# Sliding-window attention: the two half-masked key blocks of a query row packed into one row of 128 columns

## The chip, the cores and the metric

The kernel runs on one core of a Trainium2 chip. The metric is the device time of one execution in microseconds (us), the median of three runs. TensorE is the matrix engine (PE in the rows; its weight loads are PEld), VectorE is DVE, ScalarE is ACT, GpSimd is POOL, and SP issues transfers.

## The reference, cut to what matters

The whole computation is two blocks of a network over 512 tokens of width 1024, in float32. The change touches one piece of it, the attention of the second layer (`swa_sink_mixer`), which has 16 query heads of width 64, 4 key heads, a window of 128 and one learned sink logit for each head:

```python
logits = jnp.einsum('bntgrd,bnsgd->bngrts', q, kk) * scale      # 128 queries x 256 keys
logits = logits + bias                                          # by distance, per head
logits = jnp.where(mask, logits, -jnp.inf)                      # 0 <= dist < 128
m = jnp.maximum(logits.max(-1), sink)
p = jnp.exp(logits - m[..., None])
denom = p.sum(-1) + jnp.exp(sink - m)
o = jnp.einsum('bngrts,bnsgd->bntgrd', p, vv) / denom
```

A block of 128 queries sees its own block of 128 keys (those at or before the query) and the block before it (those after the query's column). Of the 256 logits of a row exactly 128 are inside the window: column s of the own block where s <= t, and column s of the block before where s > t. The first block of queries has no block before it.

## The kernel before, in words

The engines run programs of their own, each strictly in the order written, and meet at semaphores. Most of the kernel is matrix products with weights that are streamed from memory in 118 chunks of 1 MB. Float32 operands are split into a high part (ACT, L1202) and a low part (POOL, L468 and L477, four pieces to a chunk), and each product is three matmuls (L503 to L505). Between these products stand two attentions.

The sliding-window attention works in 16 units. Unit i covers two heads (index x) and two query tiles of 128 (index t; tiles 0 and 1 in even units, 2 and 3 in odd ones), so a unit has four rows of logits, each of 256 keys, for every one of the 128 partitions. What each engine does for a unit:

- PE, `sw_score(i)`: logits into PSUM pair 0 (L917). There is one such pair, so the scores of a unit wait until the maximum of the unit before has been taken (`l_ready`).
- DVE, `sw_logits(i)`: scales and adds the bias, which holds the mask too (L2103, one instruction for each tile), after a memset of the block that tile 0 has not (L2099); then the maximum of each row (L2107).
- ACT, `sw_expo(i)`: four exponentials of 257 columns, the sink's column among them, with their sums (L1503). `sw_sink` puts the sink there (L1508).
- DVE, `sw_weights(i)`: reciprocal of the sums (L2112), four multiplications of 256 columns (L2115).
- PE, `sw_turn(i)`: eight transposes into PSUM pair 1 (L930).
- ACT: copies the transposed weights to `PT` (L1534).
- PE, `sw_weigh(i)`: weights times values (L944), 12 matmuls in even units and 16 in odd ones.
- DVE, `sw_finish(b)` after every second unit: two instructions that split the output (L2123, L2125).

PE's order is written out by hand. Round u has scores of unit u+2, then pieces of other matrix products (12 matmuls of 512 columns in rounds 1 to 9; six in rounds 11 to 14; 12 in round 15; here they are called the filling; in rounds 2 and 6 it stands behind the transposes), then the transposes of unit u, then the weighing of unit u-1. Round 10 has no filling. DVE's round i is `sw_logits(i+1)`, in odd rounds `sw_finish`, `sw_weights(i)`. ACT's round i is `sw_expo(i+1)`, in rounds 1, 5 and 9 the copy of new queries (L1514), the copy of `PT`, the sink of unit i+3, and in rounds 1, 5 and 9 the high part of a weight chunk (L1202).

The bias rows with the mask are made at the start of the kernel (L1697) and brought back as `BIAS` by a transfer from L1493.

Of the kernel before, what the change touches and what calls it, by code (L numbers as in the profile page):

```python
# [22 lines left out]
F32 = mybir.dt.float32  # L23
# [68 lines left out]
def build(nc, stream, x_t, mem_t, params, consts, masks, sinks, rel_in, w_pool, out):  # L92
    bias_rows = nc.dram_tensor("bias_rows", (P, SWH, 2 * P), F32).ap()
    forget_rows = nc.dram_tensor("forget_rows", (8, T), F32).ap()
    bias_toeplitz = bass.AP(bias_rows.tensor, 0, [[SWH * 2 * P - 1, P], [2 * P, SWH], [1, 2 * P]])
# [3 lines left out]
    with ExitStack() as ctx:  # L99
# [59 lines left out]
        with ExitStack() as s:  # L159
            REL = sb("REL", [BUCKETS, SWH + 2 * P], F32, s)  # L160
            ROWS = sb("ROWS", [SWH, 2 * P], F32, s)
            ROWM = sb("ROWM", [SWH, 2 * P], F32, s)
        with ExitStack() as s:
# [13 lines left out]
            with ExitStack() as s1:  # L177
                BIAS = sb("BIAS", [P, SWH, 2 * P], F32, s1)
# [3 lines left out]
                PL = sb("PL", [P, 3, 4, 2 * P + 8], F32, s1)  # L182
                PT = sb("PT", [P, 2, 8, P], F32, s1)
# [66 lines left out]
        def bk(i):  # L250
# [41 lines left out]
            sem(n) for n in ("s_mm", "l_ready", "p_exp", "p_ready", "p_turned", "pt_ready", "pv_mm"))  # L292

# [206 lines left out]
        def _(pe):  # L500
# [331 lines left out]
            pe.wait_ge(consts_in, 64)  # L832
# [101 lines left out]
            def sw_weigh(i):  # L934
# [4 lines left out]
                for t, n in enumerate(tiles):  # L939
                    nk = min(n + 1, 2)  # L940
                    for x in range(2):
                        for kb in range(nk):
# [3 lines left out]
                                           PT[:, i % 2, 4 * x + 2 * t + kb + 2 - nk], start=kb == 0, stop=kb == nk - 1)  # L946
# [248 lines left out]
        def _(act):  # L1195
# [27 lines left out]
            act.dma_start(ROWM[:, :], rel_in[BUCKETS:BUCKETS + SWH, SWH:]).then_inc(consts_in, 16)  # L1223
# [225 lines left out]
            def ffn(n_in, n_down, layer):  # L1449
# [14 lines left out]
                if layer == 1:  # L1464
# [3 lines left out]
                    act.dma_start(INV[:, :, :], consts[:, NCON:].rearrange("p (b t) -> p b t", b=2)).then_inc(inv_loaded, 16)  # L1468
# [22 lines left out]
            def load_bias():  # L1491
                act.wait_ge(rows_stored, 16)
                act.dma_start(BIAS[:, :, :], bias_toeplitz).then_inc(bias_loaded, 16)  # L1493

            layer_norm(1, par["ffn_g"][:, 0:8], par["ffn_b"][:, 0:8], load_bias)

            def sw_expo(i):
# [3 lines left out]
                for r in range(4):  # L1501
                    row = PL[:, s, r, 0:2 * P + 1]
# [3 lines left out]
            def sw_sink(i):  # L1506
                _, b, _ = SW_UNITS[i]
                act.activation(PL[:, i % 3, :, 2 * P].rearrange("p (x t) -> p x t", t=2),  # L1508
                               SINK3[:, b // 4, :, b % 4].unsqueeze(2).broadcast_to([P, 2, 2]), ACT.Copy).then_inc(sink_put, 1)

            def sw_query(c):
                pair = bank[1] if c == 0 else bank[3]
                act.wait_ge(w_used, SQ_CHUNK[c] + 1)
                act.activation(QB[:, 2 * c:2 * c + 2], pair[:, :, :], ACT.Copy).then_inc(qb_copied, 1)  # L1514
# [139 lines left out]
        def _(dve):  # L1654
# [40 lines left out]
            dve.wait_ge(consts_in, 64)  # L1695
            dve.wait_ge(rel_mm, 1)
            dve.tensor_tensor(ROWS[:, :], bk(7)[0:SWH, 0:2 * P], ROWM[:, :], ALU.add).then_inc(rows_made, 1)  # L1697
# [388 lines left out]

            BIAS5 = BIAS[:, :, :].rearrange("p (o x b) s -> p o x b s", o=2, x=2)

            def sw_logits(i):
# [37 lines left out]
            dve.wait_ge(bias_loaded, 16)  # L2127
# [307 lines left out]
```

## Time and profile before

| | |
|---|---|
| runs | 1485.28, 1484.1, 1484.4 us; median 1484.4 us |
| span of the profiled execution | 1483.1 us, first to last instruction |
| the profiled execution's own time | not shown apart from its span; the median of the runs is 1.3 us above that span |
| PE busy | 1452.5 us (98%) |
| DVE, ACT, POOL busy | 859.6, 615.7, 482.5 us |
| the 16 units on PE | from 695.84 us (first score) to 801.56 us (first matmul behind the last weighing) |

A row of the busy list gives a share of the whole span; a stage can have another limit than the whole. Matmuls are pipelined, so neighbouring ones overlap and the duration of one is more than its distance to the next.

### The profile page before, as it was taken

To read this page: it belongs to the slowest core of one execution; us is meant where nothing else is said; L and a number is where in the kernel's file an instruction comes from. 1 tells how busy PE (TensorE), PEld (TensorE's weight loads), DVE (VectorE), ACT (ScalarE), POOL (GpSimd) and SP (SyncE) were. 2 spreads that over 40 slices of the span, in tenths; PEclk is the share of its full clock that TensorE was granted. 3 is DMA by queue.
4 is the path that set the end of the run, shared out by engine and by line. 5 is a ranking of instruction groups with operands and counts; after the bars stand their busy time and mean duration, and the time that the engine had idled before them with its cause. 6 is when DMAs were issued, how large, how long until landed. Compare 5 with 4: busy or idle time off the path is not lost.

```text
span 1483.1 us, 23698 instructions
## 1 busy us (share of the span) xinstructions
PE 1452.5 (98%) x9390; PEld 1207.6 (81%) x9390; DVE 859.6 (58%) x1261; ACT 615.7 (42%) x780; POOL 482.5 (33%) x360
## 2 busy tenths in 40 slices
PE   8999999999999999999999999999999999999999
PEld 6787887898888888899777988888888897777677
DVE  7787686576665660165686666656630374565741
ACT  5565554353223221245574442232221355655541
POOL 0000000225544545432221145445454524422222
PEclk9999999999999999999999999999999999999999
DMA  7422122403222233323102122222323312322211
GB/s 222 136 74 87 58 86 102 156 29 114 85 92 106 87 112 113 112 87 106 66 30 86 57 86 85 95 103 88 110 85 112 129 58 86 130 74 71 72 56 59
DMA packets 23601, 137.25 MB, mean 93 GB/s; under 512 B 2600, under 2 KB 5208, under 8 KB 8672
## 3 DMA queue, kind: packets, MB, share of 16 engines
q1 hardware_dynamic: 18288, 124.79, 23.9%
q10 hardware_dynamic: 5232, 11.32, 2.8%
q8 instruction: 58, 0.95, 0.3%
q14 instruction: 23, 0.19, 0.0%
HBM read 131.89 MB, written 4.21 MB: 92 GB/s over the span
## 4 chain that ended last, share of the span: by engine, by line
issue 41%; PE 27%; POOL 24%; DVE 3%; DMA 2%; ACT 1%; DVEq 1%; POOLq 0%; ACTq 0%; SPq 0%
POOL WL L468 15%; POOL WL L477 9%; PE pair L503 7%; PE pair L505 6%; PE pair L504 6%; DMA RAW<-stream 1%; PE pair L1096 1%; PE pair L1083 1%; DVE WL L1672 1%; PE pair L688 1%; PE pair L1015 1%; PE pair L1073 1%; PE pair L717 1%; ACT WH L1202 1%; DMA PAR<-params 0%
## 5 line engine op out<-in xcount | busy, mean ns | idle before, releaser
L503 PE MATMUL pair<-AH,WH 128*128 128x512 f32 (+1 forms) x1240 | 473.4, 382 | 9.4 <-DVE AL L1661 6.6
L468 POOL TENSOR_TENSOR WL<-RAW,WH 128x512 fp32r<-128x512 f32 x228 | 310.5, 1394 | 475.6 <-ACT WH L1202 475.6
L505 PE MATMUL pair<-AH,WL 128*128 128x512 f32 (+1 forms) x1240 | 462.6, 373 | 0.0
L504 PE MATMUL pair<-AL,WH 128*128 128x512 f32 (+1 forms) x1240 | 462.4, 373 | 0.0
L1202 ACT ACTIVATE WH<-RAW 128x2048 fp32r<-128x2048 f32 x106 | 202.8, 1913 | 455.5 <-PE pair L505 446.4
L477 POOL TENSOR_TENSOR WL<-RAW,WH 128x512 fp32r<-128x512 f32 x128 | 171.8, 1374 | 506.8 <-ACT WH L1202 506.8
L503 PEld LDWEIGHTS pair<-AH,WH 128*128 128x128 f32 x1240 | 233.5, 188 | 58.5 <-issue 15.9
L505 PEld LDWEIGHTS pair<-AH,WL 128*128 128x128 f32 x1240 | 233.0, 188 | 41.8
L504 PEld LDWEIGHTS pair<-AL,WH 128*128 128x128 f32 x1240 | 233.5, 188 | 41.1 <-issue 1.9
L2042 DVE TENSOR_SCALAR CA<-pair,PAR 128x512 f32<-128x512 f32 x88 | 67.3, 806 | 147.4 <-PE pair L505 144.4
L503 PE MATMUL pair<-GH,WH 128*128 (+2 forms) x416 | 148.7, 357 | 0.1
L504 PE MATMUL pair<-GL,WH 128*128 (+2 forms) x416 | 147.7, 355 | 0.0
L505 PE MATMUL pair<-GH,WL 128*128 (+2 forms) x416 | 147.7, 355 | 0.0
L2047 DVE SCALAR_TENSOR_TENSOR CA<-pair,PAR,CA 128x510 f32<-128x510 f32 (+1 forms) x176 | 123.7, 744 | 14.0 <-issue 12.1
L503 PE MATMUL pair<-OH,WH 128*128 128x512 f32 (+1 forms) x256 | 89.4, 349 | 1.8 <-POOL WL L477 0.9
L503 PEld LDWEIGHTS pair<-GH,WH 128*128 128x128 f32 x416 | 78.1, 188 | 11.8 <-POOL WL L477 0.3
L505 PEld LDWEIGHTS pair<-GH,WL 128*128 128x128 f32 x416 | 78.4, 188 | 11.2
L504 PEld LDWEIGHTS pair<-GL,WH 128*128 128x128 f32 x416 | 78.1, 188 | 11.3
L504 PE MATMUL pair<-OL,WH 128*128 128x512 f32 (+1 forms) x256 | 86.1, 336 | 0.0
L505 PE MATMUL pair<-OH,WL 128*128 128x512 f32 (+1 forms) x256 | 86.0, 336 | 0.0
L1868 DVE TENSOR_TENSOR WL<-RAW,WH 128x1024 fp32r<-128x1024 f32 x16 | 22.4, 1444 | 99.5 <-ACT WH L1216 99.0
L503 PE MATMUL pair<-WH,AH 128*128 128x256 f32 (+1 forms) x192 | 59.7, 311 | 0.8 <-DVE AL L1952 0.6
(249 smaller groups left out, 1890.4 us busy)
## 6 DMA issues: line engine op xcount, KB each, us to landing
RAW<-stream SPq DMA_DIRECT2D x114, 1024.0 KB, 4.9
H<-x_t SPq DMA_DIRECT2D x5, 512.0 KB, 6.6
bias_rows<-ROWS ACTq DMA_DIRECT2D x1, 2048.0 KB, 24.5
BIAS<-bias_rows ACTq DMA_DIRECT2D x1, 2048.0 KB, 7.8
FBC<-forget_rows ACTq DMA_DIRECT2D x4, 512.0 KB, 4.0
out<-H ACTq DMA_DIRECT2D x8, 256.0 KB, 2.0
H<-x_t SPq DMA_DIRECT2D x1, 1024.0 KB, 10.4
RAW<-stream SPq DMA_DIRECT2D x3, 256.0 KB, 6.7
```

What stands on the lines that cost most here:

```text
L468: pool.tensor_tensor(WL[w][:, part], RAW[raw][:, part], WH[w][:, part].bitcast(F32), ALU.subtract).then_inc(w_lo, 1)
L477: pool.tensor_tensor(wl[:, :, part], raw[:, :, part], wh[:, :, part].bitcast(F32), ALU.subtract).then_inc(w_lo, 1)
L503: pe.matmul(out_, wh, xh, start=start, stop=False, skip_group_check=shared)
L504: pe.matmul(out_, wh, xl, start=False, stop=False, skip_group_check=shared)
L505: return pe.matmul(out_, wl, xh, start=False, stop=stop, skip_group_check=shared)
L688: mm = pe.matmul(out_[b:b + BLK, h, c * BLK:c * BLK + BLK], k_[:, b:b + BLK], q_[:, b:b + BLK], start=True, stop=True)
L717: mm = pe.matmul(pair_a[:, h, cs], vv[:, c, h * P:h * P + P], SS[:, h, c], start=c == 0, stop=True)
L1015: pe.matmul(bk(5), con["mean64"], SQH[:, :], start=True, stop=True).then_inc(n_summed, 1)
L1202: act.activation(WH[w][:, :], RAW[raw][:, :], ACT.Copy).then_inc(w_hi, 1)
L1868: dve.tensor_tensor(WL[w][:, part], RAW[w][:, part], WH[w][:, part].bitcast(F32), ALU.subtract).then_inc(e_lo, 1)
L2042: dve.tensor_scalar(out_[:, c], src[:, c], tap[2], CONVB[:, layer, ab, blk], ALU.mult, ALU.add)
L2047: ins = dve.scalar_tensor_tensor(out_[:, c, d:T], src[:, c, 0:T - d], CONVW[:, layer, 2 - d, ab, blk], out_[:, c, d:T], ALU.mult, ALU.add)
```

## The change

A query row keeps 128 columns from the start. ACT copies the own block's logits from PSUM to `PL` (`sw_own`), DVE overwrites the columns after the query with those of the block before (a predicated copy), and then the bias, the maximum, the exponential, the division and the transposes work on 128 columns. After the transpose the packed weights are spread again into two blocks, by a multiplication with two 0/1 masks (`sw_part`, on DVE, in place of ACT's copy). The transposes of neighbouring units go to two banks of pair 1 in turn. The scale moves to the copy of the queries. The bias loses its mask and half its columns; `PM`, the two masks, is a transfer more. Tile 0's missing block comes from the constant `causal`, whose masked columns hold -1e30.

```diff
             def sw_turn(i):
                 pe.wait_ge(p_ready, i + 1)
-                if i:
-                    pe.wait_ge(pt_ready, i)
-                for t in range(2):
-                    for x in range(2):
-                        for kb in range(2):
-                            at = 2 * t + kb
-                            mm = pe.transpose(bk(2 + x)[:, at * P:at * P + P],
-                                              PL[:, i % 3, 2 * x + t, kb * P:kb * P + P], con["ident"])
+                if i >= 2:
+                    pe.wait_ge(pt_ready, i - 1)
+                for r in range(4):
+                    mm = pe.transpose(bk(2 + i % 2)[:, r * P:r * P + P], PL[:, i % 3, r, 0:P], con["ident"])
                 mm.then_inc(p_turned, 1)
...
             def load_bias():
                 act.wait_ge(rows_stored, 16)
                 act.dma_start(BIAS[:, :, :], bias_toeplitz).then_inc(bias_loaded, 16)
+                act.dma_start(PM[:, :, :], consts[:, NCON + 2 * T:].rearrange("p (k t) -> p k t", k=2)).then_inc(bias_loaded, 16)
...
-                    row = PL[:, s, r, 0:2 * P + 1]
+                    row = PL[:, s, r, 0:P + 1]
...
-            def sw_sink(i):
+            def sw_own(i):
                 _, b, _ = SW_UNITS[i]
-                act.activation(PL[:, i % 3, :, 2 * P].rearrange("p (x t) -> p x t", t=2),
+                if i >= 3:
+                    act.wait_ge(p_turned, i - 2)
+                act.activation(PL[:, i % 3, :, P].rearrange("p (x t) -> p x t", t=2),
                                SINK3[:, b // 4, :, b % 4].unsqueeze(2).broadcast_to([P, 2, 2]), ACT.Copy).then_inc(sink_put, 1)
+                act.wait_ge(s_mm, i + 1)
+                own = bank[0][:, :, :].rearrange("p x (t k s) -> p (x t) k s", t=2, k=2)[:, :, 1]
+                act.activation(PL[:, i % 3, :, 0:P], own, ACT.Copy).then_inc(own_put, 1)
...
-            for i in range(3):
-                sw_sink(i)
+            sw_own(0)
             sw_expo(0)
+            sw_own(1)
...
             for i in range(16):
                 if i + 1 < 16:
                     sw_expo(i + 1)
+                if i + 2 < 16:
+                    sw_own(i + 2)
                 if i in (1, 5, 9):
                     sw_query((i + 3) // 4)
-                act.wait_ge(p_turned, i + 1)
-                if i >= 2:
-                    act.wait_ge(pv_mm, i - 1)
-                act.activation(PT[:, i % 2].rearrange("p (x k) c -> p x (k c)", x=2), bank[1][:, :, :], ACT.Copy).then_inc(pt_ready, 1)
-                if i + 3 < 16:
-                    sw_sink(i + 3)
-                if i in (1, 5, 9):
                     split_next(SQ_CHUNK[(i + 3) // 4])
...
             def sw_logits(i):
                 _, b, tiles = SW_UNITS[i]
-                s = i % 3
-                rows = PL[:, s].rearrange("p (x t) s -> p x t s", t=2)
-                nmax = NMAX[:, s].rearrange("p (x t) -> p x t", t=2)
-                bias = BIAS5[:, b // 4, :, b % 4]
+                rows = PL[:, i % 3, :, 0:P]
+                both = rows.rearrange("p (x t) s -> p x t s", t=2)
+                before = bank[0][:, :, :].rearrange("p x (t k s) -> p x t k s", t=2, k=2)[:, :, :, 0]
+                bias = BIAS5[:, b // 4, :, b % 4].unsqueeze(2).broadcast_to([P, 2, 2, P])
+                pair = LATER.unsqueeze(1).broadcast_to([P, 2, P])
                 dve.drain()
-                if i >= 3:
-                    dve.wait_ge(p_turned, i - 2)
+                dve.wait_ge(own_put, i + 1)
                 if tiles[0] == 0:
-                    dve.memset(rows[:, :, 0, 0:P], NEG)
-                dve.wait_ge(s_mm, i + 1)
-                for t in range(2):
-                    lo = P if tiles[t] == 0 else 0
-                    dve.scalar_tensor_tensor(rows[:, :, t, lo:2 * P], bank[0][:, :, 256 * t + lo:256 * t + 256], SCALE, bias[:, :, lo:],
-                                             ALU.mult, ALU.add)
+                    dve.copy_predicated(both[:, :, 0], pair, con["causal"].unsqueeze(1).broadcast_to([P, 2, P]))
+                    dve.copy_predicated(both[:, :, 1], pair, before[:, :, 1])
+                else:
+                    dve.copy_predicated(rows, LATER.unsqueeze(1).broadcast_to([P, 4, P]), before.rearrange("p x t s -> p (x t) s"))
+                dve.drain()
+                dve.tensor_tensor(both, both, bias, ALU.add)
                 dve.drain()
                 dve.wait_ge(sink_put, i + 1)
-                dve.tensor_reduce(nmax, rows[:, :, :, 0:2 * P + 1], AX_X, ALU.max, negate=True).then_inc(l_ready, 1)
+                dve.tensor_reduce(NMAX[:, i % 3], PL[:, i % 3, :, 0:P + 1], AX_X, ALU.max, negate=True).then_inc(l_ready, 1)
...
-                for r in range(4):
-                    ins = dve.tensor_scalar(PL[:, s, r, 0:2 * P], PL[:, s, r, 0:2 * P], RDEN[:, s, r:r + 1], None, ALU.mult)
-                ins.then_inc(p_ready, 1)
+                dve.tensor_tensor(PL[:, s, :, 0:P], PL[:, s, :, 0:P], RDEN[:, s].unsqueeze(2).broadcast_to([P, 4, P]),
+                                  ALU.mult).then_inc(p_ready, 1)
+
+            def sw_part(i):
+
+                dve.wait_ge(p_turned, i + 1)
+                if i >= 2:
+                    dve.wait_ge(pv_mm, i - 1)
+                turned = bk(2 + i % 2).rearrange("p (r t) -> p r t", r=4).unsqueeze(1).broadcast_to([P, 2, 4, P])
+                dve.tensor_tensor(PT[:, i % 2], turned, PM[:, :, :].unsqueeze(2).broadcast_to([P, 2, 4, P]),
+                                  ALU.mult).then_inc(pt_ready, 1)
...
             for i in range(16):
                 if i + 1 < 16:
                     sw_logits(i + 1)
+                if i:
+                    sw_part(i - 1)
                 if i >= 3 and i % 2:
                     sw_finish((i - 3) // 2)
                 sw_weights(i)
+            sw_part(15)
             sw_finish(7)
```

## Rows read from the trace of the kernel before

**Rows 1.** The page: the span, and busy time by engine.

```profile
span 1483.1 us, 23698 instructions
...
PE 1452.5 (98%) x9390; PEld 1207.6 (81%) x9390; DVE 859.6 (58%) x1261; ACT 615.7 (42%) x780; POOL 482.5 (33%) x360
```

**Rows 2.** Stretches: busy PE, PEld, DVE, ACT, POOL; then PE's granted clock, DMA.

```profile
775.00:785.00 10.00, 7.83 (x56) 5.80 (x56) 9.29 (x19) 6.71 (x22) 3.36 (x3) 1.00 0.30 107
785.00:795.00 10.00, 9.29 (x81) 6.87 (x80) 7.04 (x16) 6.98 (x20) 0.00 (x0) 1.00 0.21 65
```

**Rows 3.** Waits in 695 to 806 us: total us, times, longest.

```profile
DVE PL L2103 <- PE pair L917: 24.0, 6, 9.8
...
PE pair L930 <- DVE PL L2115: 2.7, 5, 1.4
```

**Rows 4.** Groups by line in 695 to 806 us: busy us, mean ns, idle before.

```profile
L1503 ACT ACTIVATE PL<-PL,SMALL 128x257 f32<-128x257 f32 x64 | 31.9, 500 | 5.2 <-DVE SMALL L2107 4.3
L2115 DVE TENSOR_SCALAR PL<-PL,SMALL 128x256 f32<-128x256 f32 x64 | 22.7, 418 | 1.2
...
L2107 DVE TENSOR_REDUCE SMALL<-PL 128x4 f32<-128x1028 f32 x16 | 19.6, 1224 | 1.5 <-issue 0.4
...
L2103 DVE SCALAR_TENSOR_TENSOR PL<-pair,BIAS 128x512 f32<-128x512 f32 (+1 forms) x32 | 18.3, 613 | 25.0 <-PE pair L917 24.0 <-issue 1.0
L930 PE MATMUL pair<-CON,PL 128*128 128x128 f32 x128 | 17.0, 276 | 2.7 <-DVE PL L2115 2.7
...
L1534 ACT ACTIVATE PT<-pair 128x1024 f32<-128x1024 f32 x16 | 16.3, 1021 | 22.1 <-PE pair L930 22.1
...
L1202 ACT ACTIVATE WH<-RAW 128x2048 fp32r<-128x2048 f32 x5 | 9.5, 1910 | 0.0
...
L2125 DVE TENSOR_TENSOR OL<-pair,OH 128x512 fp32r<-128x512 f32 x8 | 5.5, 692 | 0.6
```

**Rows 5.** Timeline, rounds 4 and 10 to 15: start us, length us, instruction, idle before.

```profile
736.51 0.50 PE L503 MATMUL pair<-AH,WH 128*128 128x512 f32 x1
...
739.37 1.04 PE L930 MATMUL pair<-CON,PL 128*128 128x128 f32 x8
...
771.06 0.93 PE L917 MATMUL pair<-KT,QB 64*128 64x128 f32 x8
771.07 1.14 DVE L2115 TENSOR_SCALAR PL<-PL,SMALL 128x256 f32<-128x256 f32 x4
...
772.39 0.27 DVE L2099 MEMSET PL<- 128x256 f32 x1 [0.18 <-issue]
...
774.98 1.13 PE L917 MATMUL pair<-KT,QB 64*128 64x256 f32 x8 [0.54 <-DVE SMALL L2107]
...
801.56 0.50 PE L503 MATMUL pair<-OH,WH 128*128 128x512 f32 x1
```

**Rows 6.** Timelines of POOL and of DVE around 726 us.

```profile
726.28 5.06 POOL L468 TENSOR_TENSOR WL<-RAW,WH 128x512 fp32r<-128x512 f32 x4 [11.48 <-ACT WH L1202]
...
729.00 3.02 DVE L2115 TENSOR_SCALAR PL<-PL,SMALL 128x256 f32<-128x256 f32 x4
```

**Rows 7.** Whole span, shapes apart: instructions of the kinds that the change adds.

```profile
L1894 DVE TENSOR_TENSOR SY<-SY,H 128x512 f32<-128x512 f32 x12 | 8.3, 692 | 1.0
...
L1780 DVE TENSOR_TENSOR E<-pair,E 128x1024 f32<-128x1024 f32 x4 | 4.9, 1224 | 9.8 <-ACT E L1245 9.8
...
L2234 DVE TENSOR_REDUCE SMALL<-PL 128x2 f32<-128x512 f32 x4 | 2.7, 686 | 0.3
...
L1755 DVE COPY_PREDICATED SB<-MASK,pair 128x256 f32<-128x256 uint32 x4 | 1.8, 450 | 0.1
...
L1554 ACT ACTIVATE PL<-PL,SMALL 128x128 f32<-128x128 f32 x8 | 3.1, 395 | 0.3
...
L1617 ACT ACTIVATE PT<-pair 128x512 f32<-128x512 f32 x4 | 2.4, 598 | 17.3 <-PE pair L1083 17.3
```

**Rows 8.** The page's transfers: KB of the bias transfer, us from issue to landing.

```profile
BIAS<-bias_rows ACTq DMA_DIRECT2D x1, 2048.0 KB, 7.8
```

More of the change, by code:

```diff
@@ L94, in build @@
     forget_rows = nc.dram_tensor("forget_rows", (8, T), F32).ap()
-    bias_toeplitz = bass.AP(bias_rows.tensor, 0, [[SWH * 2 * P - 1, P], [2 * P, SWH], [1, 2 * P]])
+    bias_toeplitz = bass.AP(bias_rows.tensor, P, [[SWH * 2 * P - 1, P], [2 * P, SWH], [1, P]])
     forget_bcast = [bass.AP(forget_rows.tensor, 2 * T * j, [[0, P], [T, 2], [1, T]]) for j in range(4)]
@@ L161, in build @@
             ROWS = sb("ROWS", [SWH, 2 * P], F32, s)
-            ROWM = sb("ROWM", [SWH, 2 * P], F32, s)
         with ExitStack() as s:
@@ L177, in build @@
             with ExitStack() as s1:
-                BIAS = sb("BIAS", [P, SWH, 2 * P], F32, s1)
+                BIAS = sb("BIAS", [P, SWH, P], F32, s1)
+                sb("BIAS_GAP", [P, SWH, P], F32, s1)
                 KT = sb("KT", [P, 2, T], F32, s1)
@@ L181, in build @@
                 QB = sb("QB", [P, 8, T], F32, s1)
-                PL = sb("PL", [P, 3, 4, 2 * P + 8], F32, s1)
-                PT = sb("PT", [P, 2, 8, P], F32, s1)
+                PL = sb("PL", [P, 3, 4, P + 8], F32, s1)
+                PM = sb("PM", [P, 2, P], F32, s1)
+                sb("PM_GAP", [P, 10 * P], F32, s1)
+                PT = sb("PT", [P, 2, 2, 4, P], F32, s1)
             with ExitStack() as s1:
@@ L292, in build @@
             sem(n) for n in ("s_mm", "l_ready", "p_exp", "p_ready", "p_turned", "pt_ready", "pv_mm"))
+        own_put = sem("own_put")
         n_squared, n_summed, n_rstd, n_made = (sem(n) for n in ("n_squared", "n_summed", "n_rstd", "n_made"))
@@ L831, in _ @@
             values(0, (0, 1, 2, 3))
-            pe.wait_ge(consts_in, 64)
+            pe.wait_ge(consts_in, 48)
             for it in range(4):
@@ L945, in sw_weigh @@
                                            VT[:, n + 1 - nk + kb, c0:c0 + 64],
-                                           PT[:, i % 2, 4 * x + 2 * t + kb + 2 - nk], start=kb == 0, stop=kb == nk - 1)
+                                           PT[:, i % 2, kb + 2 - nk, 2 * x + t], start=kb == 0, stop=kb == nk - 1)
                 mm.then_inc(pv_mm, 1)
@@ L1222, in _ @@
             act.preload_act_table_set("natural_log_exp_and_others")
-            act.dma_start(ROWM[:, :], rel_in[BUCKETS:BUCKETS + SWH, SWH:]).then_inc(consts_in, 16)
             act.dma_start(REL[:, 0:SWH], rel_in[0:BUCKETS, 0:SWH]).then_inc(rel_loaded, 16)
@@ L1467, in ffn @@
                         act.activation(MH[:, 4 * half:4 * half + 4], MT[:, 4 * half:4 * half + 4], ACT.Copy).then_inc(mh_ready, 1)
-                    act.dma_start(INV[:, :, :], consts[:, NCON:].rearrange("p (b t) -> p b t", b=2)).then_inc(inv_loaded, 16)
+                    act.dma_start(INV[:, :, :], consts[:, NCON:NCON + 2 * T].rearrange("p (b t) -> p b t", b=2)).then_inc(inv_loaded, 16)
                 split_next(n_down + 7)
@@ L1513, in sw_query @@
                 act.wait_ge(w_used, SQ_CHUNK[c] + 1)
-                act.activation(QB[:, 2 * c:2 * c + 2], pair[:, :, :], ACT.Copy).then_inc(qb_copied, 1)
+                act.activation(QB[:, 2 * c:2 * c + 2], pair[:, :, :], ACT.Copy, scale=SCALE).then_inc(qb_copied, 1)
             act.wait_ge(w_used, N_KV + 1)
@@ L1694, in _ @@
             dve.tensor_scalar(LB[:, 1], LB[:, 0], -1.0, 1.0, ALU.mult, ALU.add)
-            dve.wait_ge(consts_in, 64)
+            dve.wait_ge(consts_in, 48)
             dve.wait_ge(rel_mm, 1)
-            dve.tensor_tensor(ROWS[:, :], bk(7)[0:SWH, 0:2 * P], ROWM[:, :], ALU.add).then_inc(rows_made, 1)
+            dve.tensor_copy(ROWS[:, :], bk(7)[0:SWH, 0:2 * P]).then_inc(rows_made, 1)
             dve.drain()
@@ L2125, in sw_finish @@
                 dve.tensor_tensor(ol, o, oh.bitcast(F32), ALU.subtract).then_inc(o_ready, 1)
-            dve.wait_ge(bias_loaded, 16)
+            dve.wait_ge(bias_loaded, 32)
             sw_logits(0)
@@ L2320, in constants @@
 def constants():
-    c = np.zeros((P, NCON + 2 * T), np.float32)
+    c = np.zeros((P, NCON + 2 * T + 2 * P), np.float32)
     i = np.arange(P)
@@ L2336, in constants @@
     win = np.array(POOL_WINDOWS)[(i[:, None] // 64) + 2 * np.arange(2)[None]]
-    c[:, NCON:] = (1.0 / np.minimum(np.arange(T)[None, None] + 1, win[:, :, None])).reshape(P, -1)
+    c[:, NCON:NCON + 2 * T] = (1.0 / np.minimum(np.arange(T)[None, None] + 1, win[:, :, None])).reshape(P, -1)
+    c[:, NCON + 2 * T:] = np.concatenate([i[:, None] > i[None, :], i[:, None] <= i[None, :]], axis=1)
     masks = np.zeros((P, LEVELS - 1, P), np.float32)
@@ L2345, in constants @@
     j = np.arange(2 * P)
-    dist = P - j
-    ok = (dist >= 0) & (dist < P)
-    dc = np.clip(dist, 0, P - 1)
+    dc = (-j) % P
     d = np.maximum(dc, 1).astype(np.float32)
@@ L2351, in constants @@
     bucket = np.where(dc < 16, dc, np.minimum(log_b, BUCKETS - 1))
-    hot = ((bucket[None] == np.arange(BUCKETS)[:, None]) & ok[None]).astype(np.float32)
-    return c, masks, hot, np.where(ok, 0.0, NEG).astype(np.float32)
+    hot = (bucket[None] == np.arange(BUCKETS)[:, None]).astype(np.float32)
+    return c, masks, hot
 def kernel(**inputs):
@@ L2360 @@
     a = {k: np.asarray(v) for k, v in inputs.items()}
-    con, masks, hot, row_mask = constants()
+    con, masks, hot = constants()
     parts = []
@@ L2411 @@
     params = np.concatenate([vec[n] for n, _ in PARAMS], axis=1)
-    rel_in = np.zeros((BUCKETS + SWH, SWH + 2 * P), np.float32)
-    rel_in[0:BUCKETS, 0:SWH] = a["rel_bias"]
-    rel_in[0:BUCKETS, SWH:] = hot
-    rel_in[BUCKETS:, SWH:] = row_mask
+    rel_in = np.zeros((BUCKETS, SWH + 2 * P), np.float32)
+    rel_in[:, 0:SWH] = a["rel_bias"]
+    rel_in[:, SWH:] = hot
     w_pool = np.zeros((P, 2, P), np.float32)
```

1 line of the change is left out of this document (added).

## The prediction

> **What bounds the kernel.** I read the page first: PE is busy 98% of 1483.1 us, so as a whole the kernel is PE's [rows 1]. The change lies in one stage, so I then read stretches of that stage. There PE is not always full: 7.83 of 10 us from 775, while DVE has 9.29 [rows 2]; PE's granted clock is 1.00 in both, which is 2.4 GHz. The waits come next. For most of the stage DVE waits for scores (24.0 us [rows 3]) and ACT for transposes (22.1 us [rows 4]): PE sets the pace. But PE also waits for the weights that DVE makes, five times, 2.7 us in all [rows 3], and for the maximum, as in front of the scores of unit 13 [rows 5]. The reader is to see two parts. In rounds 0 to 9 PE has much filling and is the bound. From round 10 on the filling is thin and PE and DVE hold each other up. All idle time of PE in the stage is some 5.8 us, so that is the most that smoother waits could give; anything beyond must come out of PE's own work.
>
> **The terms on PE.** Eight transposes become four. The group L930 is busy 17.0 us for 16 units [rows 4], 1.06 us each; the last matmul lasts 0.28, so the distance from one to the next is (1.06 - 0.28) / 7 = 0.11 us. Four fewer save 0.44 us, 16 times: **-7.0 us**. Scores and weighing keep their number and size. That is what the change gives if nothing else becomes late.
>
> **The terms on ACT.** Exponentials: 257 columns take 0.50 us, 128 columns 0.395 [rows 4, 7]; four cost about 0.4 us less. The `PT` copy (1.02 us [rows 4]) leaves; a copy of 512 columns from PSUM (0.60 us [rows 7]) comes. ACT loses some 0.9 us a unit and is not the bound. But the new copy has a place in the chain: it stands behind `sw_expo(i+1)` (four pieces, 1.6 us), and in rounds 1, 5 and 9 the 1.9 us split of a chunk (L1202 [rows 4]) is also ahead of it.
>
> **The terms on DVE**, for a unit:
>
> - L2103 leaves, 18.3 / 16 = 1.14 us [rows 4], and the 0.18 us of the memset in even units [rows 5].
> - A predicated copy of 512 columns comes. The trace has it at 256 columns, 0.450 us [rows 7]. Other DVE kinds need 1.04 us for 1000 columns more: (1.224 - 0.692) / 512 [rows 7]. So 0.450 + 0.27 = **0.72 us**, and 0.81 in even units, where it is two of 256 (the second overlaps by 0.09). Bounds: not below 0.45, and 0.90 if it cost 256 twice in full.
> - The bias addition comes: 0.69 us, as L1894, and a drain of 0.07.
> - The maximum goes from 1.224 [rows 4] to 0.69 us (L2234 at 512 columns [rows 7]).
> - Four multiplications (1.14 us together [rows 5]) become one of 512 columns with two operands, 0.69 us.
> - `sw_part` comes: 1024 columns from PSUM with a second operand, as L1780, 1.224 us [rows 7]; it overlaps the instruction ahead by 0.09, so 1.13.
>
> Sum: out 1.14 + 0.09 + 1.22 + 1.14 = 3.59; in 0.76 + 0.76 + 0.69 + 0.69 + 1.13 = 4.03. DVE gets 0.44 us more in each unit, where PE gets 0.44 less. With reciprocal (0.17), drains and half of `sw_finish` (two of 0.69 us [rows 4]), DVE goes from 4.8 to 5.2 us a unit. PE's unit with full filling goes from 5.75 to 5.3 (scores 0.86 or 1.06, filling 2.84 (736.51 to 739.37 [rows 5]), transposes 0.97 to 0.53, weighing 0.86 or 1.07), and with six matmuls of filling from 4.4 to 3.9. So DVE comes level with PE in rounds 1 to 9, and is well above it from round 10.
>
> **Why the waits grow by more than the sums say.** The scores have one PSUM pair and wait for the maximum. Between one unit's scores and the next stood L2103 and L2107, 2.5 us; now ACT's copy 0.60, predicated copy 0.72, addition 0.76, maximum 0.76: 2.9 us with the hand-over, and whatever ACT and DVE have in front of them. I walked the stage unit by unit: each instruction starts at the end of the one before on its engine, or 0.05 us after the last thing it waits for, with the lengths above. The same walk over the old order puts the scores of unit 12 at 770.2 us and the first matmul after the last weighing at 800.6, against 771.06 and 801.56 [rows 5], and its PE waits 0.4 us up to unit 12's scores and 5.2 after. It is a microsecond short, but has the waits where the trace has them. Three of the new waits, worked:
>
> - Transposes of unit 6. When `sw_logits(7)` is done, PE does unit 8's scores (0.86) while DVE does `sw_part(5)` 1.14, reciprocal and drain 0.17, multiplication 0.69: 2.0 us. PE waits 1.1. In round 10 it is the same.
> - Scores of unit 13. Unit 12's scores end at 771.1. ACT is in the chunk split until 771.4, then in the exponentials until 773.1, puts the sink and copies until 773.8. DVE: predicated copies 0.98 with the drain, addition 0.76 and some 0.4 behind POOL, maximum 0.76, until 776.8. PE was ready at 773.8: 3.0 us.
> - Transposes of unit 11. From 776.8 DVE has `sw_part(10)` 1.14, `sw_finish` 1.54, reciprocal and multiplication 0.86: 780.3. PE has scores and six matmuls, until 779.3: 1.0 us.
>
> Up to unit 12's scores the new waits are 0.4, 1.3, 0.7, 0.4, 1.1, 0.1, 0.6 and 0.3 us, 4.9 together against 0.4: +4.5, and ten turns save 4.4. **About 0.** From there to the end they are 1.1, 3.0, 1.0, 1.0, 1.1, 1.0, 1.6 and 0.4, 10.2 against 5.2: +5.0, and six turns save 2.6. **+2.4 us.** Behind the stage PE has products without a gap and later work shifts with it: no cover gives the 2.4 back. The last tail (transposes, spread, weigh, `sw_finish(7)`) has DVE's 1.22 for ACT's 1.02, inside the sum.
>
> **POOL.** Some of L2115's groups are longer: 3.02 instead of 1.14 us in the middle of a POOL burst of 5.06 us [rows 6]. The mean of the 64 is 418 ns [rows 4] and their busy sum 4.5 us above 16 times 1.14. Three bursts fall in the stage's paced part. Now one multiplication can be held, and the addition too, since it reads two tiles of SBUF where L2103 read PSUM and one. At most one POOL piece each, 5.06 / 4 = 1.27 us: 0 to 7.6 us over three bursts, 3.8 in the middle. I count no difference; the walk has both sides.
>
> The Trainium skill, "SBUF — State Buffer", on the ways into the memory, says that a DVE instruction in a two-port mode or with two SBUF inputs and a GpSimd one take one shared pair of ports in turn, each for its whole length. The 3.02 us agrees. By that rule alone the addition becomes exposed and the multiplication is exposed once in place of four times; the sum stays as it is.
>
> The Trainium skill, "VectorE: DVE Perf Modes", in its tier table, speaks against one edit: in float32 from SBUF a multiplication by a scalar takes two elements a cycle, one with two tensors one. By rate alone 1024 columns at two and 512 at one cost the same, and the edit gives nothing. The rows show 1.14 against 0.69, since the four pay a fixed part four times. By the rule DVE would have 0.45 us more a unit, and the walk comes to about +6.
>
> **What costs nothing.** The bias transfer is issued in the middle of the layer norm ahead of the attention and took 7.8 us for 2 MB [rows 8]; half the bytes and a small `PM` behind it are there before the first scores. The extra issue stands on ACT, which waits for DVE in that norm; if uncovered it would cost some 0.3 us. ACT's first transfer and the mask addition at the start go; they were under other waits. The scale in the query copy is free.
>
> **The rivals.**
>
> - *PE's saving stays (faster).* If DVE's new instructions overlap better than I charge, PE keeps its pace: at the full -7.0 us 1477.4 us, with half of it 1481. For it: DVE waits 24.0 us for scores in the stage before [rows 3]. Against it: these waits lie in the first part, and with every new DVE length at 0.6 the walk still gives only -0.3. 12% for more than 3 us, 6% for a smaller gain.
> - *The predicated copy or the spread costs more (slower).* It stands between one unit's scores and the next, without cover. At 1.0 us the walk gives +4.0, with 1.25 +9; `sw_part` at 1.5 instead of 1.13 gives +4.8. It decides from about 0.80 us on. With POOL at its worst +3 more. Time 1489 to 1494. 17%.
> - *Nothing moves,* since the stage's filling takes up what changes: 1484.4. Against it: every wait above is PE's. 5%.
>
> **The numbers.** Forecast, 60%: DVE takes the pace, +1 to +4.5, likeliest 1484.4 + 2.4 = **1486.8 us**; by the profiled execution 1483.1 + 2.4 = 1485.5 us of span, with the same 1.3 us around it. 0.2% is 3.0 us, about what the measurement tells from no change. Of the forecast's 60%, 22 lie above +3.0. Slower 22 + 17 = 39%, faster 12%, same 49%. The range leaves out the full saving and the far end of the second rival: 1482.2 to 1491.5. The forecast's own range is 1485.4 to 1488.9.
>
> **What would show it.** L930's group busy 9 to 10 us; DVE busy above 9 of 10 us from unit 10 on; PE waiting for the maximum and for the weights some 15 us in place of 5.8; unit 12's scores near where they were, first matmul after the last weighing near 804.0; `sw_part` 1.22 us, the predicated copy 0.72. Wrong would be a DVE that still waits 20 us for PE behind unit 2, or predicated copies of 1 us.

## The result and the profile after

The changed kernel takes 1487.51 us (median of 18 runs, 1485.86 to 1491.98), the kernel before 1484.53 (18 runs). The ratio is 1.0018, 95% interval [1.0011, 1.0025]: some 2.7 us slower (the two medians are 3.0 us apart), which is more than the measurement is uncertain, but under the 0.2% that I had set for a difference.

The page of the changed kernel, span and busy time, against [rows 1] (the profiled execution itself took 1487.26 us):

```profile
span 1485.4 us, 23546 instructions
...
PE 1446.1 (97%) x9326; PEld 1200.6 (81%) x9326; DVE 865.9 (58%) x1229; ACT 602.0 (41%) x780; POOL 485.0 (33%) x360
```

PE is busy 6.4 us less and the span is 2.3 us longer, so in the whole span PE is idle 8.7 us more. Groups by line between 695 and 812 us, shapes apart; against [rows 4]:

```profile
L1502 ACT ACTIVATE PL<-PL,SMALL 128x129 f32<-128x129 f32 x64 | 25.0, 393 | 38.6 <-DVE SMALL L2109 38.3
L2125 DVE TENSOR_TENSOR PT<-pair,PM 128x1024 f32<-128x1024 f32 x16 | 19.5, 1217 | 2.2 <-PE pair L930 2.1
...
L2106 DVE TENSOR_TENSOR PL<-PL,BIAS 128x512 f32<-128x512 f32 x16 | 13.9, 870 | 1.2
...
L2116 DVE TENSOR_TENSOR PL<-PL,SMALL 128x512 f32<-128x512 f32 x16 | 11.1, 693 | 1.6 <-issue 0.4
L2109 DVE TENSOR_REDUCE SMALL<-PL 128x4 f32<-128x516 f32 x16 | 11.1, 691 | 1.2
L930 PE MATMUL pair<-CON,PL 128*128 128x128 f32 x64 | 10.4, 287 | 4.6 <-DVE PL L2116 4.6
...
L1514 ACT ACTIVATE PL<-pair 128x512 f32<-128x512 f32 x16 | 9.4, 587 | 4.1 <-PE pair L920 4.1
L2101 DVE COPY_PREDICATED PL<-CON 128x256 f32<-128x256 uint32 x8 | 6.0, 747 | 23.8 <-ACT PL L1514 23.8
L2104 DVE COPY_PREDICATED PL<-CON,pair 128x512 f32<-128x512 uint32 x8 | 5.9, 735 | 5.1 <-ACT PL L1514 4.6
```

Two things have changed their place. ACT now waits 38.3 us for the maximum, where before it waited for transposes. And DVE no longer waits for PE's scores but for ACT's copy of them (L1514). PE's waits, same stretch; they were 2.7 us for the weights [rows 3], and three of 0.31, 0.54 and 0.80 us for the maximum (L2107):

```profile
PE pair L920 <- DVE SMALL L2109: 6.0, 5, 3.5
...
PE pair L930 <- DVE PL L2116: 4.6, 5, 1.3
```

The longest is the one that the prediction worked out, in front of unit 13's scores. PE's timeline (start, length, idle before), against [rows 5]:

```profile
770.67 0.93 PE L920 MATMUL pair<-KT,QB 64*128 64x128 f32 x8
...
777.74 2.08 PE L920 MATMUL pair<-KT,QB 64*128 64x256 f32 x8 [3.54 <-DVE SMALL L2109]
779.75 0.79 PE L506 MATMUL pair<-OH,WH 128*128 128x512 f32 x1
...
782.47 1.05 PE L930 MATMUL pair<-CON,PL 128*128 128x128 f32 x4
783.46 1.27 PE L943 MATMUL pair<-PT,VT 128*64 128x128 f32 x12
784.66 0.93 PE L920 MATMUL pair<-KT,QB 64*128 64x128 f32 x8
...
804.06 0.50 PE L506 MATMUL pair<-OH,WH 128*128 128x512 f32 x1
```

Up to unit 12's scores the stage is 0.4 us shorter than before (770.67 against 771.06, with a start at 695.88 against 695.84); from there to the first matmul behind the last weighing it is 33.4 against 30.5 us. So the whole loss lies in rounds 10 to 15. There is something in it that I had not foreseen: scores that took 1.13 us take 2.08. The same place in windows (columns as in [rows 2]; the third from the end is PE's granted clock):

```profile
775.00:785.00 10.00, 7.26 (x36) 5.33 (x38) 9.21 (x15) 3.83 (x18) 2.96 (x2) 0.66 0.29 105
785.00:795.00 10.00, 9.20 (x70) 6.52 (x66) 8.75 (x14) 3.61 (x17) 0.00 (x0) 1.00 0.01 2
...
779.00:781.00 2.00, 2.00 (x7) 1.16 (x6) 1.85 (x4) 0.98 (x4) 0.00 (x0) 0.50 0.77 283
781.00:783.00 2.00, 2.00 (x7) 1.51 (x7) 1.76 (x4) 0.00 (x0) 0.00 (x0) 0.50 0.52 217
```

Behind the 3.54 us of idle PE the granted clock falls to 0.50, that is 1.2 GHz, and is back at 1.00 from 785 on. And what held unit 13's scores is seen on ACT and DVE:

```profile
770.40 1.90 ACT L1201 ACTIVATE WH<-RAW 128x2048 fp32r<-128x2048 f32 x1
772.39 0.40 ACT L1502 ACTIVATE PL<-PL,SMALL 128x129 f32<-128x129 f32 x1
...
774.04 0.57 ACT L1514 ACTIVATE PL<-pair 128x512 f32<-128x512 f32 x1
```

```profile
774.65 0.53 DVE L2101 COPY_PREDICATED PL<-CON 128x256 f32<-128x256 uint32 x1 [2.23 <-ACT PL L1514]
775.08 0.43 DVE L2102 COPY_PREDICATED PL<-CON,pair 128x256 f32<-128x256 uint32 x1
775.59 1.24 DVE L2106 TENSOR_TENSOR PL<-PL,BIAS 128x512 f32<-128x512 f32 x1
776.91 0.69 DVE L2109 TENSOR_REDUCE SMALL<-PL 128x4 f32<-128x516 f32 x1
```

Unit 12's scores are done at 771.6, and DVE is free at 772.4. But ACT first ends the split of a chunk, then does four exponentials of unit 11, and copies unit 12's own block only at 774.04. DVE stands still for 2.23 us in the middle of the stretch in which it has most to do.

### The profile page after: what moved, and what is told of

It reads as the page before. It is cut to its first block, busy times and chain, and to the rows that moved or that the text cites. A ratio compares the mean times of both kernels' runs of the same rounds, so it can differ in the third digit from the quotient of the medians.

```text
span 1485.4 us, 23546 instructions
## 1 busy us (share of the span) xinstructions
PE 1446.1 (97%) x9326; PEld 1200.6 (81%) x9326; DVE 865.9 (58%) x1229; ACT 602.0 (41%) x780; POOL 485.0 (33%) x360
## 4 chain that ended last, share of the span: by engine, by line
issue 41%; PE 26%; POOL 24%; DVE 3%; DMA 2%; ACT 1%; DVEq 1%; POOLq 0%; ACTq 0%; SPq 0%
POOL WL L471 15%; POOL WL L480 9%; PE pair L506 7%; PE pair L508 6%; PE pair L507 6%; DMA RAW<-stream 1%; PE pair L1095 1%; PE pair L1082 1%; DVE WL L1672 1%; PE pair L691 1%; PE pair L1014 1%; PE pair L1072 1%; PE pair L720 1%; ACT WH L1201 1%; DMA PAR<-params 0%
```

## The experiments

Theory 1 is that of the prediction: DVE, with ACT's copy in front of it, sets the times, and the 7.0 us that PE saves turn into waits. Its numbers come from the walk through the stage that the prediction describes, with one edit at a time. The rivals stand in each expectation; in the later ones theory 2 is that the clock's fall is itself the loss.

All ratios are to the kernel before, run on the same chip (e1 to e10 over five rounds). Its own median there was 1485.2 us for e1 to e4, 1485.0 for e5 to e8 and 1484.7 for e9 and e10, so kernels are compared by their ratios, not by their medians. "Stage" is the time from the first score matmul of unit 0 to the first matmul behind unit 15's weighing, in the one profiled execution; it leaves out what happens earlier in the kernel, where profiled executions differ by some microseconds (the stage began between 694.97 and 699.65). It was 105.72 us before and is 108.18 in the changed kernel.

| kernel | median us | ratio, 95% interval | stage us | stage against the changed kernel | the walk |
|---|---|---|---|---|---|
| before | 1484.5 | 1 | 105.72 | -2.5 | -2.4 |
| changed | 1487.5 | 1.0018 [1.0011, 1.0025] | 108.18 | 0 | 0 |
| e1 eight transposes | 1490.2 | 1.0028 [1.0017, 1.0038] | 110.61 | +2.4 | +2.2 |
| e2 half the spread | 1483.1 | 0.9985 [0.9974, 0.9995] | 104.20 | -4.0 | about -3 |
| e3 own copy first | 1484.0 | 0.9989 [0.9979, 1.0000] | 103.85 | -4.3 | -4.3 |
| e4 early release | 1488.9 | 1.0020 [1.0008, 1.0033] | 107.12 | -1.1 | -0.4 |
| e5 three edits of order | 1482.4 | 0.9979 [0.9969, 0.9989] | 102.32 | -5.9 | -5.2 |
| e6 filling in round 10 | 1489.1 | 1.0024 [1.0013, 1.0035] | 107.81 | -0.4 | 0.0 |
| e7 e5 and e6 together | 1482.3 | 0.9976 [0.9966, 0.9986] | 102.33 | -5.9 | -5.2 |
| e8 own first, new DVE order | 1483.0 | 0.9979 [0.9970, 0.9988] | 103.23 | -5.0 | -4.3 |
| e9 kernel before, reordered | 1485.3 | 1.0002 [0.9993, 1.0011] | 105.75 | | |
| e10 e8 with eight transposes | 1486.1 | 1.0006 [0.9997, 1.0015] | 105.93 | -2.3 | -1.8 |

**e1, eight transposes.** PE's saving is taken back, and nothing else.

```diff
-                for r in range(4):
+                for r in (0, 1, 2, 3, 0, 1, 2, 3):
```

> Undoes PE's saving alone: four transposes are issued twice to the same places, so the transposes cost PE 0.44 us more a unit, 7.0 us over 16 units, and nothing else changes. Theory 1 (DVE and the chain from scores to maximum set the pace, PE has waits to put them in): PE's waits shrink and the end moves by some 2 us, so about 1489.7 us against 1487.5 of the changed kernel, 3.5 per thousand over the kernel before. Theory 2 (PE is still the bound of the stage and something outside it made the change slower): the whole 7.0 us comes back, 1494.5 us.

The stage is 2.4 us longer than the changed kernel's, not 7.0. In the table's terms: the new work on DVE and ACT alone costs 4.9 us against the kernel before, and the four transposes fewer give 2.4 of it back. The other 4.6 us of PE's saving are idle time.

**e2, half the spread.** `sw_part` writes the own block only; the block before stays zero, so its weights are missing from the result.

```diff
...
-                dve.tensor_tensor(PT[:, i % 2], turned, PM[:, :, :].unsqueeze(2).broadcast_to([P, 2, 4, P]),
+                dve.tensor_tensor(PT[:, i % 2, 1], turned, PM[:, 1].unsqueeze(1).broadcast_to([P, 4, P]),
...
+            dve.memset(PT[:, :, :, :, :], 0.0)
```

> Takes half of one cost on DVE away: the spread after the transposes writes only the own block, 512 columns in place of 1024, 0.5 us less a unit (8.5 us over the stage). The block before is left out of the result (its weights are set to zero once, ahead of the first unit). Theory 1 (DVE sets the pace): about 3 us come back, 1484.5 us, level with the kernel before. Theory 2 (PE is the bound): within 0.5 us of the changed kernel, 1487.5. [...]

```profile
L2125 DVE TENSOR_TENSOR PT<-pair,PM 128x512 f32<-128x512 f32 x16 | 10.9, 683 | 2.3 <-PE pair L930 2.3
```

DVE has 0.53 us less in a unit, 8.5 us in all, and 4.0 of these come out of the stage. DVE's length does pace it, and more than the walk has it (about 3). By the ratios it is more still, 0.9985 against 1.0018, some 4.9 us.

**e3, own copy first.** ACT copies the own block of unit i+2 before the exponentials of unit i+1. No engine has less to do.

```diff
-                if i + 1 < 16:
-                    sw_expo(i + 1)
                 if i + 2 < 16:
                     sw_own(i + 2)
+                if i + 1 < 16:
+                    sw_expo(i + 1)
```

> Changes the order on ACT alone: the copy of the own block of unit i+2 stands ahead of the exponentials of unit i+1 in place of behind them (also out of the way of the 1.6 us that they take). No work is added or removed. Theory 1a (the chain scores, own copy, predicated copy, addition, maximum with what stands ahead of it on ACT costs the waits): DVE no longer waits for the copy in even units, 4.3 us come back, 1483.2 us, a little under the kernel before; PE's waits in the stage from 15.7 to 11.4 us. Theory 1b (DVE's length alone does it): at most 1 us. The exponentials come later by the copy's 0.6 us, which costs nothing while DVE has the spread and the split of the output ahead of them.

This was the sharpest of the runs: 4.3 us of stage, as the walk gives, and 0.9989 against 1.0018. PE's waits were to go from 15.7 to 11.4 us by the walk; the rows have 12.3 and 9.0. DVE's waits for the own copy from 724 to 812 us, first in the changed kernel, then here:

```profile
DVE PL L2101 <- ACT PL L1514: 8.0, 6, 2.7
```

```profile
DVE PL L2101 <- ACT PL L1514: 1.7, 3, 0.9
```

And two windows of this kernel:

```profile
775.00:785.00 10.00, 7.77 (x44) 5.74 (x45) 9.28 (x14) 3.81 (x17) 3.44 (x3) 0.83 0.31 105
785.00:795.00 10.00, 7.64 (x58) 5.20 (x56) 9.29 (x15) 5.11 (x24) 0.00 (x0) 1.00 0.09 22
```

Here DVE is full, at 9.28 and 9.29 of 10 us, with PE at 7.7. In the changed kernel the same two windows have 9.21 and 8.75, and the one before them, 765 to 775, has 7.22 against 8.80 here: that is where DVE stood still, because ACT's copy stood behind the exponentials.

**e4, early release.** The scores' PSUM pair is free behind the predicated copy instead of behind the maximum.

```diff
-                    pe.wait_ge(l_ready, i)
+                    pe.wait_ge(row_taken, i)
...
-                    dve.copy_predicated(both[:, :, 1], pair, before[:, :, 1])
+                    dve.copy_predicated(both[:, :, 1], pair, before[:, :, 1]).then_inc(row_taken, 1)
...
```

The last `...` stands for the same signal behind the odd units' predicated copy.

> Lets PE write the next scores as soon as the predicated copy has read the bank, 1.5 us sooner than behind the maximum; nothing else changes. If the wait of the scores for the maximum is by itself what costs, the scores' waits (6.0 us plus 3.9 in the weight loads) mostly go and 3 to 5 us come back: 1483 to 1484.5 us. If the own copy behind the exponentials is the next thing late (they wait for the maximum too), only 0.4 us come back: 1487.1 us. I expect the second; the walk over the stage gives it.

By the ratio (1.0020 against 1.0018) nothing comes of it; the stage has 1.1 us less in one execution, where the walk had 0.4, and the interval can neither show nor exclude that. The wait has moved. In front of unit 13's scores it is 1.50 us, for the predicated copy, in place of 3.54; in front of the transposes it was 4.6 us, and here

```profile
PE pair L930 <- DVE PL L2116: 9.3, 7, 2.8
```

PE's scores come earlier, and PE then waits for the weights, since DVE's work is the same.

**e5 to e8.** e5 is e3 and e4 with one edit more, DVE's order in a round; e8 is the same without e4; e6 moves six matmuls of filling into PE's 3.54 us of idle time, alone, and e7 does it on top of e5.

```diff
                 if i + 1 < 16:
                     sw_logits(i + 1)
-                if i:
-                    sw_part(i - 1)
                 if i >= 3 and i % 2:
                     sw_finish((i - 3) // 2)
                 sw_weights(i)
+                if i:
+                    sw_part(i - 1)
```

```diff
...
-                if u == 11:
-                    sw_mixed(0, (0,))
...
                     pe.wait_ge(o_ready, 10)
+                    sw_mixed(0, (0,))
```

> The changed kernel with three edits of order: ACT copies the own block of unit i+2 ahead of the exponentials of unit i+1; the scores' PSUM pair is released behind the predicated copy instead of behind the maximum; and DVE's round is logits, finish, weights, spread instead of logits, spread, finish, weights. Theory 1 (DVE's work between one unit's scores and the next, and in front of the weights, sets the pace, and PE's saving shows when it is out of the way): the walk puts it 5.2 us under the changed kernel, so 3 us under the kernel before: ratio 0.998 (0.997 to 0.999), 1482. Scores of unit 13 start without a wait near 771, the waits sit at the transposes of units 11 and 13 and at the weighings (0.3 to 0.6 us each). Theory 2 (the clock's fall behind the idle PE carries the loss): the same sign, but then the gain over the kernel with the own copy first alone should be over 2 us, since the 2 to 3 us of idle PE in front of unit 13's scores goes. By theory 1 it is 0.9 us.

> The changed kernel with one edit on PE: the six matmuls of filling of round 11 move to the end of round 10, in front of unit 13's scores, where PE is idle for 3.54 us. DVE's chain is the same. Theory 1 (DVE sets the times from round 10 on): the idle time is filled but the transposes of unit 11 wait that much longer; the walk gives 0.0 us, ratio 1.0018, first matmul behind the last weighing at 804.1. Theory 2 (the fall of the granted clock to 1.2 GHz behind the idle time is itself a loss of 1 to 2 us): the idle piece shrinks to about 2 us, the clock stays higher in 775 to 785, and the kernel comes 1 to 2 us under the changed one: ratio 1.0005 to 1.0012.

> The three edits of order together with the filling of round 11 moved into round 10. Theory 1: by the walk the same as the three edits alone (0.0 us between them), ratio 0.998. Theory 2 (the clock): where the three edits alone still show a fall of the granted clock, this one is up to 1 us faster than they are.

> Own copy first, and DVE's round as logits, finish, weights, spread; the scores' pair is released by the maximum as in the changed kernel. The walk puts it 4.3 us under the changed kernel, the same as the own copy first alone, so 2 us under the kernel before: ratio 0.9989 (0.998 to 1.000). If the early release is worth nothing in company either, the three edits measure the same as this one; by the walk they are 0.9 us better.

e5, e7 and e8 are all faster than both kernels, by 0.21 to 0.24% against the one before, and can't be told from one another. The early release is all that e5 has over e8. The two ratios are the same, 0.9979, but the stage is 0.9 us shorter, which is what the walk has; like the 1.1 us of e4, that is in one execution of each and is too small for the intervals. Over e3, e5 gains 1.5 us, by the stage and by the ratios: the walk had 0.9, and the theory of the clock over 2. The new DVE order gives 0.6 us of stage over e3, and by the two ratios 1.5 us; the walk had 0.0, and the intervals of e3 and e8 overlap.

e5 and e7 bear most on the clock, because in its profiled execution one has the fall and the other has not, and because the filling that e7 moves stands, in both places, ahead of the slow stretch. In both, unit 11's transposes start 79.55 us from the stage's start; from there on both have the same instructions in the same order. Windows of e5, then of e7:

```profile
775.00:785.00 10.00, 7.87 (x59) 5.69 (x58) 9.17 (x16) 3.65 (x17) 1.03 (x1) 0.83 0.30 105
```

```profile
775.00:785.00 10.00, 8.02 (x64) 5.49 (x63) 9.18 (x16) 4.97 (x22) 0.00 (x0) 1.00 0.24 96
```

Their stages are 102.32 and 102.33 us. Where the lost time went is seen on PE, e5 first:

```profile
779.52 1.65 PE L920 MATMUL pair<-KT,QB 64*128 64x128 f32 x8
782.62 0.60 PE L930 MATMUL pair<-CON,PL 128*128 128x128 f32 x4
...
787.16 0.66 PE L930 MATMUL pair<-CON,PL 128*128 128x128 f32 x4 [0.22 <-DVE PL L2116]
```

```profile
776.51 0.93 PE L920 MATMUL pair<-KT,QB 64*128 64x128 f32 x8
778.87 0.66 PE L930 MATMUL pair<-CON,PL 128*128 128x128 f32 x4
...
784.83 0.66 PE L930 MATMUL pair<-CON,PL 128*128 128x128 f32 x4 [1.03 <-DVE PL L2115]
```

From the stage's start, unit 12's transposes are at 85.3 us in e5 and at 83.9 in e7, 1.4 us apart; unit 13's are at 89.85 and 89.86. The slow clock made PE's work longer and its next waits shorter: 0.22 in place of 1.03 us at unit 13's transposes, and none in place of 0.48 at the weighing of unit 11. DVE did not notice: its weights of unit 13 (L2116, L2115 in e7) start at 89.10 and 89.11 us. So in this order the fall of the clock is no loss.

e6 can't decide it for the changed kernel, though it was built to. Its idle piece shrinks to 1.87 us, but its clock falls as long: 0.78 and 0.87 in the two windows from 775 and from 785, where the changed kernel has 0.66 and 1.00. A wait of 1.75 us for unit 11's transposes takes the place of what the idle piece lost, the stage is 0.4 us shorter, and the ratio is no better. The rows of the changed kernel itself say more, ACT first, then DVE:

```profile
785.63 0.60 ACT L1514 ACTIVATE PL<-pair 128x512 f32<-128x512 f32 x1 [0.36 <-PE pair L920]
```

```profile
780.44 0.69 DVE L2116 TENSOR_TENSOR PL<-PL,SMALL 128x512 f32<-128x512 f32 x1
...
786.26 0.45 DVE L2101 COPY_PREDICATED PL<-CON 128x256 f32<-128x256 uint32 x1 [0.62 <-ACT PL L1514]
```

Unit 11's weights are ready at 781.13, and PE comes to their transposes at 782.47; at full clock it would have waited there (the same scores and filling take 2.6 us from 788.63 on, which from 777.74 gives 780.3). But the scores of unit 14 come late by it, ACT waits 0.36 us for them, and DVE 0.62 us for ACT's copy. From there to unit 14's weights DVE has no gap and PE waits for it. So by these rows the clock costs the changed kernel some 0.4 us (an estimate: ACT's 0.36) of its 2.5, and theory 2, that the fall is the loss, does not hold.

**e9, the kernel before, reordered.** The control: is it the packing that gives the gain, or order alone? The kernel before gets the early release and the order logits, weights, finish.

```diff
-                    pe.wait_ge(l_ready, i)
+                    pe.wait_ge(row_taken, i)
...
+                ins.then_inc(row_taken, 1)
...
+                sw_weights(i)
                 if i >= 3 and i % 2:
                     sw_finish((i - 3) // 2)
-                sw_weights(i)
```

> The kernel before, with the same kind of edits of order and no packing: the scores' PSUM pair is released behind the bias instruction instead of behind the maximum, and DVE's round is logits, weights, finish. Theory 1 (the gain of the reordered kernels is PE's saving of 7 us, set free by taking work out of DVE's and ACT's way): the kernel before has only some 6 us of waits in the stage and its DVE is less loaded, so the walk gives -0.6 us: ratio 0.9996 (0.999 to 1.0005). Rival (the gain is that of a better order alone, and the packing adds nothing): the kernel before gains the same 3 us, ratio 0.998.

Ratio 1.0002 and a stage of 105.75 us, where the walk had 0.6 us less: these two edits together do nothing for it. It is not the same set of edits. The own copy first has no counterpart there; the kernel before has little of such a wait (from 724 to 812 us its DVE waits 2.0 us for scores, where the changed kernel's waits 8.0 us for the copy). And its own order, logits, finish, weights, is already the one that e5 to e8 take over, so e9's order is a different edit, and not a free one: DVE waits 4.1 us for exponentials (L2114) from 724 on, which the kernel before does not, and three of its groups of multiplications take 3.2 us beside POOL (3.02, 2.17 and 2.49 before). e9 is 0.8 us ahead of the kernel before at unit 12's scores and has lost that by the end. The early release alone was not tried on the kernel before. What order can give there has a bound, its 5.8 us of waits on PE.

**e10, e8 with eight transposes**, the edit of e1 on the better kernel.

> The kernel with the own copy first and DVE's round logits, finish, weights, spread, with eight transposes in a unit again (the last four repeat the first four into the same places). Theory 1: what four transposes save is PE's time, and it shows once DVE is out of the way; the walk puts this 2.5 us above the same kernel with four transposes, where it puts the changed kernel 2.2 us under its own version with eight: ratio about 0.9996 (0.999 to 1.0005), stage from the first scores to the first matmul behind the last weighing 2.5 us longer. Rival (the transposes lie off the path in the reordered kernel too): ratio 0.998, no longer stage.

The stage goes from 103.23 to 105.93 us, 2.7 against the walk's 2.5, and the ratio from 0.9979 to 1.0006, which is 4.0 us and above the 0.9996 that was expected. With it the packed kernel is back at the kernel before: e8's gain over it is no more than the shorter transposing gives, and 4.3 of its 7.0 us still don't show in the stage.

## Why the prediction was right, and where it was off

- **The forecast.** +2.4 us was forecast, the ratio gives +2.7 (1.6 to 3.7), the stage +2.46. The first matmul behind the last weighing was to come near 804.0 and came at 804.06. The mechanism holds: PE saves, the chain between one unit's scores and the next gets longer, and the difference comes from round 10 on. e1, e2 and e3 each took out one part and moved the stage by 2.4, 4.0 and 4.3 us, where the walk has 2.2, 3 and 4.3.
- **PE's term.** 7.0 us of work was right: a turn goes from 1.04 to 0.60 us, L930's busy time from 17.0 [rows 4] to 10.4 us (9 to 10 was foretold). Nine turns take 0.60 us, six take 0.66, five of these behind a wait, and one at the slow clock takes 1.05.
- **DVE's term.** Predicated copy of 512 columns 0.735 us (0.72), maximum 0.691 (0.69), multiplication 0.693 (0.69), spread 1.217 (1.22). The addition was 0.693 alone, but five of 16 took 1.24 to 1.28 behind POOL: 0.55 to 0.59 us more each, where I had "some 0.4", and at most one piece of 1.27. That one multiplication of 512 columns would cost as much as four of 256, which the prediction also weighed, did not happen (0.693 against 1.14 us).
- **POOL's term.** "I count no difference" put this term at nothing, and the rows show one. In the three bursts of the paced part the multiplications had been held for 4.3 us in all (3.02, 2.17 and 2.49 against 1.14 three times). Now no multiplication meets a burst, the three additions are held for 1.7 us and the three predicated copies from the constant for 0.6: 2.0 us less on DVE. How much of that shows in the stage was not measured.
- **The split of the +2.4.** I had +4.5 of waits against -4.4 up to unit 12's scores, so 0, and it was -0.4; from there +2.4, and it was +2.9. PE's waits came to 4.1 and 7.0 us, not to 4.9 and 10.2 (and for the kernel before the rows have 0.6 and 4.1, where the walk has 0.4 and 5.2). The missing 3 us are the waits of 1.0, 1.0 and 1.1 us at unit 11's transposes and the scores of 14 and 15: PE did not wait there because it ran at 1.2 GHz, and its work was some 3 us longer instead. The clock was read as 1.00 in [rows 2] and taken to stay. That step was wrong, and the sum came out right because the slow clock took the place of waits, but for the some 0.4 us that reached DVE. That 2.4 and 2.46 lie so close is in part luck: the two halves are off by 0.4 and 0.5 us in opposite directions.
- **DVE's share.** "DVE above 9 of 10 us from unit 10 on" was half wrong: 9.21, but then 8.75, and 7.22 in 765 to 775. PE's waits of "some 15 in place of 5.8" came to 12.3. DVE waited 8.0 us for ACT's copy from 724 on. The prediction had the place of that copy in its 3.0 us for unit 13's scores, but summed it up as "DVE takes the pace". By e3 the place of the copy was worth 4.3 us, more than the whole loss.
- **The rivals.** "PE's saving stays" was wrong as the kernel stands, but a part of it can be had: with the own copy first and the new order (e8) the packed kernel is 3 us faster than the one before. "The predicated copy costs more" did not happen (0.735 us, under its point of 0.80).
- **Small.** Twelve matmuls of filling take 2.86 us by the two rows that the prediction names, not 2.84; nothing hangs on it.
- **What costs nothing.** The bias transfer took 5.9 us for 1 MB and held nothing; none of PE's waits in the stage is for it.

What stays open is what the order edit of DVE itself gives (e3 against e8: 0.6 us of stage) and what the early release gives (0.9 and 1.1 us of stage, in one execution each); both are too small for the timed runs here. Why the clock fell in e5 and not in e7 is open too, and so is what an early release alone would give the kernel before.

## What to carry to other kernels

When an edit moves work between engines, price the place of each new instruction in its engine's queue as well as its length: here a copy of 0.59 us cost 4.3 us because it stood behind exponentials that nobody needed so soon, and the swap of two pieces of ACT's order turned a loss of 0.2% into a time level with the kernel before or 0.1% under it (0.9989, with 1.0000 the end of its interval). The freed time of an engine shows only up to where the next engine's chain begins; putting the freed work back (eight transposes again) measures how much of it shows, 2.4 of 7.0 us here. And a slow clock or an idle piece is a loss only as far as another engine comes to wait for it: compare the place where the next wait ends, not the lengths. In e5 nothing came to wait; in the changed kernel DVE did, for some 0.4 us.

## What the runs showed of the hardware that was not expected

- PE's granted clock fell from 1.00 to 0.50 (2.4 to 1.2 GHz) behind an idle piece of 3.54 us, and was back some 7 us later; eight score matmuls took 2.08 in place of 1.13 us. The length of the idle piece in front does not tell by itself whether it falls: the clock in 775 to 785 was 0.83 behind 4.38 us in e2, 0.83 behind 1.66 us in e5, and 1.00 behind 1.74 us in e7. The fall cost nothing that can be seen in e5, and some 0.4 us in the changed kernel (the estimate above).
- The predicated copy from a constant (L2101, 256 columns) waits for POOL like the addition does: 0.45 us when POOL is idle, 1.36, 1.33, 0.56, 0.83 and 0.53 in POOL's five bursts. The prediction priced it as the copy from PSUM [rows 7]. The Trainium skill, "SBUF — State Buffer", section "Who interferes with whom", says that a DVE instruction with two SBUF inputs and a GpSimd one that reads SBUF keep each other waiting; this copy reads its mask and its constant from SBUF, and the trace agrees. The copy of 256 columns whose source is in PSUM (L2102) took 0.43 to 0.44 us in the same five bursts; the one of 512 columns (L2104, at most 0.75 us) never met a burst.
